# The mixed heads' norm in pieces beside the latent heads and the output projection, and the input projection's 32-token tile in four f32 parts

## The chip, the cores and the metric

The kernel runs on one core of one Trainium2 chip, as one launch that reads and writes HBM. The time is device microseconds of that core, as the median of the runs shown. The core has a matrix engine (PE, TensorE), whose weight loads are traced apart (PEld), a vector engine (DVE), a scalar engine (ACT), a general engine (POOL, GpSimd) and an engine that only issues transfers here (SP). Each has its own instruction queue and works it off in order; they meet at semaphores.

## The reference

One step of a streaming encoder with two layers. 1024 frames of a new stream and 32 frames of a running one make 1056 tokens of 1024 features. Cut to what matters:

```python
h = rmsnorm(x)                          # per token over 1024 features
cols = h @ w_in                         # 9 blocks of 246 columns: inputs of three kinds of heads
y_fox, y_swa, y_mla = ...               # attention; 6, 6 and 4 heads of 64 features
y = concat(rms(y_fox), rms(y_swa), rms(y_mla)) * g_mix_out     # "mixed heads' norm": each kind by itself
x = x + y @ w_out
x = x + ConvFFN(rmsnorm(x))             # 1024 -> 2816 -> 1024
# _rmsnorm: x * rsqrt(mean(x * x) + 1e-6) * g, all in float32
```

## The kernel before

Everything lies transposed in SBUF where it is multiplied: features on the 128 partitions in 8 chunks (`DC`), tokens along the free axis, in three thirds of 352 tokens (`NT`, `TN`). In the input projection tokens are taken in nine tiles: eight of 128 and one of 32 (the running stream's; number `QT` = 8). A product in nearly full precision is made of three reduced-precision (fp32r) matmuls: each operand is split into a high part (a copy that rounds, on ACT) and a low part (value minus high part, on POOL or DVE), and high x high, high x low and low x high are added in PSUM.

A layer is a row of stages, each an `nc.Block`, which ends when all engines are through with it. Inside, each engine's program is written out by hand, and semaphores order them. The stages of a layer: `ProjectIn` (w_in in 9 steps of 246 columns); `fox_rows`, `attend_prompt` and `attend_sample` for fox, then for swa; `mla_prepare`, which builds queries, keys and values of the latent (MLA) heads; `attend_prompt` and `attend_sample` for MLA, whose results are chunks 6 and 7 of `yT`; `restart`, in which POOL clears the semaphores for use by the next stages; `norm`; and `layer_out`, which holds `ProjectOut`, `ConvFFN` and, in layer 0, the next layer's `ProjectIn`, in one Block.

`ProjectIn` loads a block of raw weights per step (SP, `load`, L487 to L492; two buffers), ACT makes its high part (`split`, L509), POOL its low part (`low`, L500), and PE runs 8 chunks x 3 matmuls for each of nine tiles (L546). ACT evicts each tile scaled by its token's root (L523).

`norm` handles the three groups (fox is chunks 0 to 2, swa 3 to 5, MLA 6 to 7) third by third: squares on ACT and POOL, sums over partitions by a matmul with ones on PE (L395), Ln and Exp on ACT, scaling on DVE (L412), high part on ACT, low part on DVE and POOL. Its SP also starts the loads of w_out's first two blocks:

```python
    restart(nc, used)
    ...
        norm(nc, k, yT, y_hi, y_lo, k.vec[lay], V_GM, "2" + k.tag, [(0, 3), (3, 6), (6, 8)], first_blocks)
```

`ProjectOut` takes w_out in 8 blocks (`m`) x three thirds x 24 matmuls (L1807). Its ACT and POOL split a block (L1721, L1728); SP loads the blocks, and brings and stores the residual x.

At the end of layer 0's FFN, `Tail` makes the next layer's operand as columns of x are finished: for each of 24 pieces (128x352) DVE adds the last product (L2143) and, one piece later, makes a low part (`Tail.low_part`, L2206); ACT makes the high part and a square, POOL adds the squares. PE's next work is the first step of layer 1's `ProjectIn`.

## Time and profile before

| what | value |
|---|---|
| median of 3 runs | 3323.86 us (3323.02 to 3326.49) |
| the profiled execution's own time | 3319.49 us |
| its span | 3317.7 us |
| PE busy | 2993.8 us, 90% of the span |
| PEld / DVE / ACT / POOL busy | 84% / 47% / 30% / 26% |
| mean granted TensorE clock | 0.935 of full speed |

The stages and durations quoted later are from the profiled execution; it was 4.37 us shorter than the median. The busy share of PE is an average: most of the rest of the span lies in stretches in which PE waits for a stage's other engines.

### The profile page before, as it was taken

To read this page: it belongs to the slowest core of one execution; us is meant where nothing else is said; L and a number is where in the kernel's file an instruction comes from. 1 tells how busy PE (TensorE), PEld (TensorE's weight loads), DVE (VectorE), ACT (ScalarE), POOL (GpSimd) and SP (SyncE) were. 2 spreads that over 40 slices of the span, in tenths; PEclk is the share of its full clock that TensorE was granted. 3 is DMA by queue.
4 is the path that set the end of the run, shared out by engine and by line. 5 is a ranking of instruction groups with operands and counts; after the bars stand their busy time and mean duration, and the time that the engine had idled before them with its cause. 6 is when DMAs were issued, how large, how long until landed. Compare 5 with 4: busy or idle time off the path is not lost. (4 is left out here: it accounts for less than half of the span.)

```text
span 3317.7 us, 50480 instructions
## 1 busy us (share of the span) xinstructions
PE 2993.8 (90%) x19996; PEld 2799.5 (84%) x19996; DVE 1575.9 (47%) x2735; ACT 992.2 (30%) x2175; POOL 860.9 (26%) x488
## 2 busy tenths in 40 slices
PE   7998877677999999999999998867679999999998
PEld 6997755456999999999899975636479999999998
DVE  3336655734344444444441474657333444444443
ACT  4224535534311111111232253445433111111111
POOL 3112141113422232223331123311143232222230
PEclk9998968788999999999999997788889999999999
DMA  5110100002511111111131101000034111111111
GB/s 182 37 42 22 40 11 18 1 9 63 169 58 38 51 50 38 40 49 43 51 102 47 41 2 40 10 17 1 13 98 149 51 38 51 38 51 38 51 51 53
DMA packets 181248, 161.79 MB, mean 49 GB/s; under 512 B 17236, under 2 KB 168316, under 8 KB 180860
## 3 DMA queue, kind: packets, MB, share of 16 engines
q1 hardware_dynamic: 181116, 160.02, 15.6%
q8 instruction: 84, 1.38, 0.2%
q14 instruction: 48, 0.39, 0.0%
HBM read 129.97 MB, written 30.13 MB: 48 GB/s over the span
## 5 line engine op out<-in xcount | busy, mean ns | idle before, releaser
L1954 PE MATMUL bank_b<-x_hi,fwhi 128*128 128x352 f32 x2112 | 690.1, 327 | 5.3 <-POOL fwlo L1910 5.3
L1954 PE MATMUL bank_b<-x_hi,fwlo 128*128 128x352 f32 x2112 | 688.4, 326 | 0.0
L1954 PE MATMUL bank_b<-x_lo,fwhi 128*128 128x352 f32 x2112 | 686.7, 325 | 0.0
L1910 POOL TENSOR_TENSOR fwlo<-raw,fwhi 128x1024 fp32r<-128x1024 f32 x132 | 321.9, 2439 | 583.3 <-ACT fwhi L2035 569.2
L1954 PEld LDWEIGHTS bank_b<-x_hi,fwhi 128*128 128x128 f32 x2112 | 399.4, 189 | 6.5 <-POOL fwlo L1910 5.9
L1954 PEld LDWEIGHTS bank_b<-x_lo,fwhi 128*128 128x128 f32 x2112 | 401.7, 190 | 0.0
L1954 PEld LDWEIGHTS bank_b<-x_hi,fwlo 128*128 128x128 f32 x2112 | 398.4, 189 | 0.6
L2143 DVE TENSOR_TENSOR fx<-fx,bank_b 128x352 f32<-128x352 f32 x528 | 275.3, 521 | 233.5 <-PE bank_b L1984 233.5
L1984 PE MATMUL bank_b<-fuhi,fwhi 128*128 128x352 f32 x1056 | 344.1, 326 | 10.2 <-DVE fx L2143 5.7
L1984 PE MATMUL bank_b<-fulo,fwhi 128*128 128x352 f32 x1056 | 344.5, 326 | 0.0
L1984 PE MATMUL bank_b<-fuhi,fwlo 128*128 128x352 f32 x1056 | 344.0, 326 | 0.0
L2055 ACT ACTIVATE fuhi<-fcb 128x1024 fp32r<-128x1024 f32 x44 | 46.7, 1061 | 696.4 <-PE bank_b L1984 550.8
L1919 POOL TENSOR_TENSOR fcb<-fcb,rsb 128x1024 f32<-128x1024 f32 x44 | 97.0, 2203 | 511.2 <-ACT fcb L2049 511.2
L1984 PEld LDWEIGHTS bank_b<-fuhi,fwhi 128*128 128x128 f32 x1056 | 201.3, 191 | 13.9 <-DVE fx L2143 8.9
L1984 PEld LDWEIGHTS bank_b<-fulo,fwhi 128*128 128x128 f32 x1056 | 199.0, 188 | 0.0
L1984 PEld LDWEIGHTS bank_b<-fuhi,fwlo 128*128 128x128 f32 x1056 | 198.6, 188 | 0.0
L546 PE MATMUL bank_a<-whi,x_hi 128*128 128x246 f32 (+1 forms) x648 | 181.9, 281 | 13.5 <-POOL x_lo L321 11.3
L546 PE MATMUL bank_a<-whi,x_lo 128*128 128x246 f32 (+1 forms) x648 | 182.0, 281 | 0.0
L546 PE MATMUL bank_a<-wlo,x_hi 128*128 128x246 f32 (+1 forms) x648 | 182.0, 281 | 0.0
L546 PE MATMUL bank_b<-whi,x_lo 128*128 128x246 f32 (+1 forms) x648 | 180.6, 279 | 0.0
L546 PE MATMUL bank_b<-wlo,x_hi 128*128 128x246 f32 (+1 forms) x648 | 180.5, 278 | 0.0
L546 PE MATMUL bank_b<-whi,x_hi 128*128 128x246 f32 (+1 forms) x648 | 179.8, 277 | 0.1
(410 smaller groups left out, 5965.8 us busy)
## 6 DMA issues: line engine op xcount, KB each, us to landing
raw<-in_w_ffn_up SPq DMA_DIRECT2D x88, 512.0 KB, 3.9
raw<-in_w_ffn_down SPq DMA_DIRECT2D x44, 512.0 KB, 3.6
wraw<-in_w_in SPq DMA_DIRECT2D x18, 984.0 KB, 5.4
xs<-x_between SPq DMA_DIRECT2D x16, 528.0 KB, 4.1
x_between<-xs SPq DMA_DIRECT2D x16, 528.0 KB, 2.6
fx<-x_between SPq DMA_DIRECT2D x2, 4224.0 KB, 13.3
raw<-in_w_out SPq DMA_DIRECT2D x16, 512.0 KB, 5.3
x_between<-fx SPq DMA_DIRECT2D x3, 1408.0 KB, 6.3
```

Of the source, the lines that this page charges most:

```text
L546: last = pe.matmul(bank[0:n, t % NB, 0:WN], a[:, c, at], w[b][:, c, :], start=(c == 0 and m == 0), stop=(c == DC - 1 and m == 2))
L1910: pool.tensor_tensor(self.wlo[:, r], self.raw[:, o % 2], self.whi[:, r].bitcast(F32), ALU.subtract)\
L1919: pool.tensor_tensor(v, v, self.rsb[:, 0:SEQ], ALU.mult)
L1954: last = pe.matmul(bank[:, first_bank + t, 0:TN], w[:, role, c, :], x[:, c, self.cols(t)], start=(c == 0 and m == 0), stop=(c == DC - 1 an ...
L1984: last = pe.matmul(bank[:, 6 + o % 2, 0:TN], w[:, D0 + e, m, :], x[:, e, self.cols(t)], start=(e == 0 and i == 0), stop=(e == 1 and i == 2))
L2055: act.activation(uhi[:, e, 0:SEQ], cb[:, e, 0:SEQ], ACT.Copy)
L2143: dve.tensor_tensor(x, x, bank[:, 6 + o % 2, 0:TN], ALU.add).then_inc(self.p_out[o % 2], 1)
```

## The change

**Norm.** The stage `norm` goes, in both layers. A class `MixedNorm` does its work in other stages. The first six chunks (fox and swa): POOL squares and adds them in `mla_prepare` (10 instructions of 128x1056, `pool_squares`), followed there by 6 sums on PE and Ln and Exp on ACT. In the stage of `attend_prompt` for MLA 18 pieces (6 chunks x 3 thirds) are scaled on DVE, get a high part on ACT and a low part on POOL, one piece for each unit (head and block of queries) of the 24 units. The last two chunks (MLA's own result) are squared, summed, scaled and split at the beginning of `layer_out`, while PE multiplies chunks 0 to 5 for `m` = 0 and 1. The loads and splits of w_out's first two blocks move into `attend_sample` for MLA. `restart` moves from behind that stage to between `mla_prepare` and `attend_prompt` (it clears 97 semaphores instead of 103).

**Input projection.** The 32-token tile is multiplied in full-precision f32: the weights are the raw block `wraw`, its 246 columns in four parts of 62, 62, 62 and 60 (`PARTS`) that go to four groups of 32 PSUM partitions. An f32 matmul shows as two records in a trace, so there are 8 x 4 x 2 = 64 records where there were 24. The operand is high plus low part of the 32 tokens, added up by `vector_samples` on DVE. The raw buffer is now read by PE, so SP's next load waits for PE's last tile too. ACT evicts the tile in four pieces. PE's queue at the last tile of step 0, where `tok_lo` is the tokens' low parts and `win_tf2` a free PSUM bank; before (these three rows stand eight times):

```order
L546 MATMUL bank_a<-whi_90,x_hi 32x246 [waits win_tf2,tok_lo]
L546 MATMUL bank_a<-wlo_92,x_hi 32x246
L546 MATMUL bank_a<-whi_90,x_lo 32x246
```

and now (the last two rows repeat to the end of the tile):

```order
L595 MATMUL bank_a<-wraw_89,const 32x62 [waits win_xs,win_tf2,tok_lo]
L595 MATMUL bank_a<-wraw_89,const 32x62 x2
L595 MATMUL bank_a<-wraw_89,const 32x60
L595 MATMUL bank_a<-wraw_89,const 32x62 x3
L595 MATMUL bank_a<-wraw_89,const 32x60
```

The 32 tokens' operand (in `const`) comes from DVE (`win_xs`), and four parts follow each other for each chunk. SP's queue at the loads of w_in for steps 2 to 8 of layer 0, before (a loop; `win_lo0` says that a block's low part is made):

```order
L492 ISA [waits win_lo0]
L492 DMA wraw_88<-in_w_in 128x8x246
L492 ISA [waits win_lo1]
L492 DMA wraw_89<-in_w_in 128x8x246
L475 REGISTER_ALU
L475 COMPARE_AND_BRANCH
L492 DMA wraw_88<-in_w_in 128x8x246 [waits win_lo0]
```

and now (seven such rows, written out, and behind them the first load of another stage):

```order
L530 DMA wraw_89<-in_w_in 128x8x246 [waits win_done2,win_lo0]
L530 DMA wraw_90<-in_w_in 128x8x246 [waits win_done2,win_lo1]
...
L779 DMA fcl_55<-in_cache_fox_logf 128x8x6
```

Each load now also waits for `win_done2`, the end of the 32-token tile two steps before the one loaded, whose weights lie in the same buffer. PE's queue from the end of MLA's sample stage to the output projection, before:

```order
L1397 MATMUL psO_smla<-pT_smla,vm 128x64 x17
L1320 UNCONDITIONAL_BRANCH
L386 UNCONDITIONAL_BRANCH [waits barrier_Pool_Activation_PE_DVE_SP_release]
L395 MATMUL nps_0<-nsq_0,const 128x352 [waits norm_sq]
...
L351 UNCONDITIONAL_BRANCH
L2317 UNCONDITIONAL_BRANCH [waits barrier_Pool_Activation_PE_DVE_SP_release]
L1807 MATMUL bank_b<-y_hi_7907,fwhi_8056 128x352 [waits wout_lo0]
```

and now:

```order
L1467 MATMUL psO_smla<-pT_smla,vm 128x64 x17
L1384 UNCONDITIONAL_BRANCH
L2426 UNCONDITIONAL_BRANCH [waits barrier_Pool_Activation_PE_DVE_SP_release]
L1893 MATMUL bank_b<-y_hi_2114,fwhi_2123 128x352 [waits wout_lo0]
...
L468 MATMUL bank_b<-ylsq_2120,const 128x352 [waits mix_p] x2
L468 MATMUL bank_b<-ylsq_2120,const 128x352 [waits mix_ln,mix_p]
L1893 MATMUL bank_b<-y_hi_2114,fwhi_2123 128x352 [waits wout_lo1]
...
L1893 MATMUL bank_b<-y_hi_2114,fwhi_2123 128x352 [waits mix_lo]
```

The norm's sums and one barrier are gone from between the two stages; the last group's sums (L468) stand between the chunks 0 to 5 of `m` = 0 and those of `m` = 1, and the late chunks wait for that group's low parts (`mix_lo`).

**Places.** Buffers move: the residual x and the FFN's input low part lie elsewhere, and `Tail`'s low parts of the first third are made 16 adds behind (`BEHIND`) and those of the other two thirds after all adds (`vector_third`), each third after its x is stored.

The diff, cut to its core:

```diff
+    def pool_squares(self, pool):
+        own = Steps(pool, self.pool_steps, self.steps0)
+        for g, acc in enumerate(self.acc):
+            a, b, c = (self.y[:, 3 * g + n, :] for n in range(3))
+            own.after(pool.tensor_tensor(acc[:, :], a, a, ALU.mult))
+            own.after(pool.tensor_tensor(self.sq[0][:, :], b, b, ALU.mult))
+            own.after(pool.tensor_tensor(self.sq[1][:, :], c, c, ALU.mult))
+            own.after(pool.tensor_tensor(acc[:, :], acc[:, :], self.sq[0][:, :], ALU.add))
+            own.after(pool.tensor_tensor(acc[:, :], acc[:, :], self.sq[1][:, :], ALU.add))
...
+    def sums(self, pe, banks):
+        for n in range(self.GROUPS * NT):
+            g, t = divmod(n, NT)
+            pe.wait_ge(self.pool_steps, self.steps0 + 5 * (g + 1))
+            if n >= 2:
+                pe.wait_ge(self.logged, self.sums0 + n - 1)
+            pe.matmul(banks[:, n % 2, 0:TN], self.k.const[:, C_ONE:C_ONE + P], self.acc[g][:, self.cols(t)],
+                      start=True, stop=True).then_inc(self.summed, 1)
+    def scalar_roots(self, act, banks):
+        for n in range(self.GROUPS * NT):
+            g, t = divmod(n, NT)
+            act.wait_ge(self.summed, self.sums0 + n + 1)
+            act.activation(self.roots[:, g, self.cols(t)], banks[:, n % 2, 0:TN], ACT.Ln, scale=1.0 / (3 * P),
+                           bias=self.k.const[:, C_EPS:C_EPS + 1]).then_inc(self.logged, 1)
+        act.wait_ge(self.logged, self.sums0 + self.GROUPS * NT)
+        act.activation(self.roots[:, :, :], self.roots[:, :, :], ACT.Exp, scale=-0.5).then_inc(self.rooted, 1)
...
+    def vector(self, dve, n):
+        if 0 <= n < self.PIECES:
+            c, at = self.piece(n)
+            v = self.y[:, c, at]
+            dve.scalar_tensor_tensor(v, v, self.gain[:, c:c + 1], self.roots[:, c // 3, at], ALU.mult, ALU.mult)\
+                .then_inc(self.normed, 1)
+    def scalar(self, act, n):
+        if 0 <= n < self.PIECES:
+            c, at = self.piece(n)
+            act.wait_ge(self.normed, self.pieces0 + n + 1)
+            act.activation(self.hi[:, c, at], self.y[:, c, at], ACT.Copy).then_inc(self.hi_done, 1)
+    lowered = 0
+    def pool_upto(self, pool, upto):
+        for n in range(self.lowered, min(upto, self.PIECES)):
+            c, at = self.piece(n)
+            pool.wait_ge(self.hi_done, self.pieces0 + n + 1)
+            if n:
+                pool.wait_ge(self.lo_done, self.pieces0 + n)
+            pool.tensor_tensor(self.lo[:, c, at], self.y[:, c, at], self.hi[:, c, at].bitcast(F32), ALU.subtract)\
+                .then_inc(self.lo_done, 1)
+            self.lowered = n + 1
...
+    def last_scalar(self, act, bank):
+        k = self.k
+        for t in range(NT):
+            act.activation(self.last_sq[:, 0, self.cols(t)], self.y[:, self.EARLY, self.cols(t)], ACT.Square)\
+                .then_inc(self.act_sq, 1)
+        for t in range(NT):
+            act.wait_ge(self.summed, self.last_sums0 + t + 1)
+            act.activation(self.last_roots[:, self.cols(t)], bank[:, 6 + t % 2, 0:TN], ACT.Ln, scale=1.0 / (2 * P),
+                           bias=k.const[:, C_EPS:C_EPS + 1]).then_inc(self.logged, 1)
+        act.wait_ge(self.logged, self.last_sums0 + NT)
+        act.activation(self.last_roots[:, :], self.last_roots[:, :], ACT.Exp, scale=-0.5).then_inc(self.rooted, 1)
+        for n, t, c in self.last_pieces():
+            act.wait_ge(self.normed, self.last0 + n + 1)
+            act.activation(self.hi[:, c, self.cols(t)], self.y[:, c, self.cols(t)], ACT.Copy).then_inc(self.hi_done, 1)
...
+    def last_vector(self, dve):
+        for t in range(NT):
+            y = self.y[:, self.EARLY + 1, self.cols(t)]
+            dve.tensor_tensor(self.last_sq[:, 1, self.cols(t)], y, y, ALU.mult).then_inc(self.dve_sq, 1)
+        dve.wait_ge(self.rooted, self.roots0 + 2)
+        for n, t, c in self.last_pieces():
+            v = self.y[:, c, self.cols(t)]
+            dve.scalar_tensor_tensor(v, v, self.gain[:, c:c + 1], self.last_roots[:, self.cols(t)], ALU.mult, ALU.mult)\
+                .then_inc(self.normed, 1)
+        for n, t, c in self.last_pieces():
+            dve.wait_ge(self.hi_done, self.last0 + n + 1)
+            dve.tensor_tensor(self.lo[:, c, self.cols(t)], self.y[:, c, self.cols(t)],
+                              self.hi[:, c, self.cols(t)].bitcast(F32), ALU.subtract).then_inc(self.lo_done, 1)
...
+    PARTS = [(32 * g, 62 * g, min(62 * (g + 1), WN)) for g in range(4)]
...
-        def body(i, b, step):
-            if is_first(i):
-                return
+        for step in range(2, WSTEPS):
+            i, b = divmod(step, 2)
             sp.wait_ge(self.lo_done[b], i)
+            sp.wait_ge(self.tile_done[QT % self.NB], (step - 1) * self.per)
             sp.dma_start(self.raw[b][:, :, :], w_in_block(self.k, self.lay, step)).then_inc(self.raw_in[b], 16)
-        self.steps(sp, body)
...
-                act.activation(proj[0:n, t, col:col + WN], self.bank[0:n, t % NB, 0:WN], ACT.Copy,
-                               scale=k.rs1[0:n, t:t + 1]).then_inc(self.tile_free[t % NB], 1)
+                parts = [(0, 0, WN)] if t < QT else self.PARTS
+                for p, a, z in parts:
+                    last = act.activation(proj[0:n, t, col + a:col + z], self.bank[p:p + n, t % NB, 0:z - a], ACT.Copy,
+                                          scale=k.rs1[0:n, t:t + 1])
+                last.then_inc(self.tile_free[t % NB], 1)
...
+                    if t == QT:
+                        if c == 0 and is_first(step):
+                            pe.wait_ge(self.samples_in, 1)
+                        for p, a, z in self.PARTS:
+                            last = pe.matmul(bank[p:p + n, t % NB, 0:z - a], self.samples[:, c, :],
+                                             self.raw[b][:, c, a:z], start=(c == 0), stop=(c == DC - 1))
+                        continue
...
+                if beside:
+                    pool.wait_ge(pool_normed, len(shared))
+                    beside.pool_upto(pool, NU)
...
+                    if beside:
+                        beside.scalar(act, m - 3)
...
+                if weights:
+                    weights.load_w(sp, 0)
+                    weights.load_w(sp, 1)
...
+                pool.wait_ge(zeroed, 4)
+                mixed.pool_squares(pool)
...
+    def slot(self, m):
+        return m if m < 2 else 2 + m % 2
+    def split_behind(self, m):
+        return (2,) if m == 0 else (3,) if m == 1 else (m + 1,) if 3 <= m < DC - 1 else ()
...
+        early, late = range(mixed.EARLY), range(mixed.EARLY, DC)
+        for m in range(2):
+            pe.wait_ge(self.lo_w[m], 1)
+            for t in range(NT):
+                third(m, t, early)
+            if m == 0:
+                mixed.last_sums(pe, bank)
+        for m in range(2):
+            for t in range(NT):
+                mixed.last_split(pe, t)
+                third(m, t, late).then_inc(self.tile_done[m], 1)
+        for m in range(2, DC):
             b = m % 2
             pe.wait_ge(self.lo_w[b], m // 2 + 1)
             for t in range(NT):
-                if m >= 2:
-                    pe.wait_ge(self.added[b], (m // 2 - 1) * NT + t + 1)
-                at = slice(t * TN, (t + 1) * TN)
-                for c in range(DC):
...
     def low_part(self, dve, o):
         m, at = self.place(o)
+        if m == 0:
+            dve.wait_ge(self.x_stored[o // DC], 16)
         dve.wait_ge(self.hi_done, o + 1)
+        dve.wait_ge(self.squared, o + 1)
         dve.scalar_tensor_tensor(self.k.lo[:, m, at], self.ffn.xT[:, m, at], self.gain[:, m:m + 1],
                                  self.k.hi[:, m, at].bitcast(F32), ALU.mult, ALU.subtract).then_inc(self.lo_done, 1)
     def vector(self, dve, o):
-        if o:
-            self.low_part(dve, o - 1)
-        if o == self.O - 1:
+        if o >= self.BEHIND:
+            self.low_part(dve, o - self.BEHIND)
+    def vector_third(self, dve, t):
...
                 else:
                     ffn.vector(dve, lambda o: tail.vector(dve, o))
+                    tail.vector_third(dve, 1)
                     front.vector(dve)
+                    tail.vector_third(dve, 2)
+                    dve.wait_ge(tail.lo_done, tail.O)
+                    pin.vector_samples(dve)
...
+        mla_prepare(nc, k, lay, places, proj, qm, km, vm, mixed)
+        restart(nc, used)
         left.close()
-        attend_prompt(nc, k, "mla", MLAH, MQK, lambda h: qm[:, :, h, :], lambda h: km[:, :, h, :],
-                      lambda h, t: vm[:, t, h, :], lambda h: h, yT, 6)
+        with ExitStack() as f2:
+            keep(f2, "y_early", mixed.EARLY * places.CHUNK)
+            attend_prompt(nc, k, "mla", MLAH, MQK, lambda h: qm[:, :, h, :], lambda h: km[:, :, h, :],
+                          lambda h, t: vm[:, t, h, :], lambda h: h, yT, 6, beside=mixed)
...
-    restart(nc, used)
-    y_lo = places.at("y_lo" + k.tag, [P, DC, TOK], places.XT, F32R)
-    y_hi = places.at("y_hi" + k.tag, [P, DC, TOK], places.Y_HI, F32R)
-    raw = places.at("raw" + k.tag, [P, 2, DC, P], places.RAW)
-    def first_blocks(sp):
-        for b in range(2):
-            sp.dma_start(raw[:, b], w_out_block(k, lay, b)).then_inc(k.sems["wout"]["raw"][b], 16)
-    with ExitStack() as f:
-        keep(f, "y_kept", places.LOW)
-        norm(nc, k, yT, y_hi, y_lo, k.vec[lay], V_GM, "2" + k.tag, [(0, 3), (3, 6), (6, 8)], first_blocks)
+                      [], yT, 6, weights=pout)
     right.close()
```

## Rows read from the trace of the kernel before

**Rows 1.** The page: engines' busy time; POOL's 128x1024 additions (busy us, mean ns).
```profile
PE 2993.8 (90%) x19996; PEld 2799.5 (84%) x19996; DVE 1575.9 (47%) x2735; ACT 992.2 (30%) x2175; POOL 860.9 (26%) x488
...
L1919 POOL TENSOR_TENSOR fcb<-fcb,rsb 128x1024 f32<-128x1024 f32 x44 | 97.0, 2203 | 511.2 <-ACT fcb L2049 511.2
```

**Rows 2.** Windows: input projection, MLA prompt, norm, output projection, MLA sample.
```profile
core 0: us, PE busy (x) PEld busy (x) DVE busy (x) ACT busy (x) POOL busy (x), PEclk, DMA share, GB/s
65.00:264.00 199.00, 199.00 (x1723) 198.23 (x1722) 72.09 (x89) 52.73 (x90) 31.69 (x7) 1.00 0.17 51
617.00:705.00 88.00, 80.55 (x672) 69.41 (x672) 55.91 (x120) 48.80 (x135) 10.03 (x8) 0.91 0.00 1
733.00:785.00 52.00, 17.16 (x48) 10.26 (x48) 23.66 (x28) 29.03 (x29) 18.33 (x7) 0.66 0.12 31
785.00:881.00 96.00, 95.54 (x579) 95.55 (x580) 28.77 (x46) 29.69 (x53) 40.73 (x32) 0.97 0.39 123
724.00:728.00 4.00, 4.00 (x18) 3.88 (x18) 0.00 (x0) 0.00 (x0) 0.00 (x0) 0.50 0.00 0
```

**Rows 3.** Timeline, MLA prompt to output projection: start, us, instruction, [idle before].
```profile
705.11 0.28 ACT L1164 ACTIVATE yT<-psOmla 128x128 f32<-128x128 f32 x1 [2.20 <-PE psOmla L1117]
...
707.36 0.34 PE L1344 MATMUL psQ_smla<-const,qm 32*96 32x32 f32 x4 [2.29 <-PEq L2364]
...
732.51 0.41 DVE L1480 COPY yT<-psO_smla 64x32 f32<-64x32 f32 x2 [3.81 <-PE psO_smla L1397]
...
742.69 0.99 SPq L2496 DMA_DIRECT2D raw<-in_w_out  x2
...
756.89 4.97 PE L395 MATMUL nps<-nsq,const 128*128 128x352 f32 x16 [0.56 <-ACT nsq L362]
...
759.52 1.28 ACT L372 ACT_TABLE_LOAD   x1
760.82 1.08 ACT L372 ACTIVATE nrs<-nrs 128x1056 f32<-128x1056 f32 x1
...
761.93 0.58 DVE L412 SCALAR_TENSOR_TENSOR nhf<-yT,vec,nrs 128x352 f32<-128x352 f32 x1 [2.36 <-ACT nrs L372]
...
785.46 0.66 PE L1807 MATMUL bank_b<-y_hi,fwhi 128*128 128x352 f32 x1 [23.59 <-POOL fwlo L1728]
```

**Rows 4.** Waits between 617 and 705 us: waiting, releaser, us in total, times, longest.
```profile
ACT qThimla L1127 <- PE psXmla L1053: 27.3, 13, 14.4
...
DVE stmla L1198 <- PE psSmla L1084: 17.5, 18, 2.4
```

**Rows 5.** Timeline of POOL and DVE in `mla_prepare`.
```profile
603.94 5.54 POOL L1536 TENSOR_TENSOR km<-km,mhs 128x3072 f32<-128x3072 f32 x1 [51.20 <-ACT mhs L1545]
604.22 8.88 DVE L1630 TENSOR_TENSOR qm<-qm,mhs 128x3456 f32<-128x3456 f32 x1
613.13 3.76 DVE L1631 TENSOR_TENSOR qm<-qm,row 128x3456 f32<-128x3456 f32 x1
```

**Rows 6.** Timeline of PE where it makes f32 products of few columns.
```profile
703.11 1.97 PE L1117 MATMUL psOmla<-pTmla,vm 128*64 128x128 f32 x32 [0.83 <-ACT pTmla L1143]
...
715.65 1.98 PE L1371 MATMUL psS_smla<-kT_smla,qz_smla 96*32 96x352 f32 x24 [0.33 <-issue]
...
723.99 4.26 PE L1397 MATMUL psO_smla<-pT_smla,vm 128*128 128x64 f32 x18 [0.58 <-DVE pT_smla L1303]
```

**Rows 7.** Timeline of ACT in the input projection, at the turn of a step.
```profile
215.11 1.83 ACT L509 ACTIVATE whi<-wraw 128x1968 fp32r<-128x1968 f32 x1
...
217.53 0.47 ACT L523 ACTIVATE proj<-bank_a,rs 128x246 f32<-128x246 f32 x1 [0.59 <-PE bank_a L546]
```

**Rows 8.** The view of line L492, SP's w_in loads: from issue to landing.
```profile
DMA to landing us min/median/max: 5.1/5.4/9.6
```

**Rows 9.** Timeline of the FFN's last matmuls in layer 0, with what POOL did.
```profile
1645.22 4.34 POOL L500 TENSOR_TENSOR wlo<-wraw,whi 128x1968 fp32r<-128x1968 f32 x1 [5.93 <-ACT whi L509]
...
1650.42 0.66 PE L1984 MATMUL bank_b<-fuhi,fwhi 128*128 128x352 f32 x1 [4.88 <-DVE fx L2143]
```

279 lines of the change are left out of this document (132 added, 147 removed).

## The prediction, made before the changed kernel had run

> **What bounds the kernel now.** I read the page first: PE is busy 90% of the span [rows 1], so a gain comes either from PE's own work or from the stretches in which PE waits for other engines. The windows tell these apart [rows 2]. In the input projection (65 to 264 us) PE is busy without a break at full granted clock: 1723 matmuls in 199 us, 115.5 ns each. What shortens PE's work there shortens the kernel. The output projection (785 to 881 us) is just as full. Between 733 and 785 us, the norm, no engine is busy for more than 29 of 52 us: the stage is a chain through all of them. In the MLA prompt stage (617 to 705 us) PE is busy for 80.6, DVE 55.9, ACT 48.8, POOL 10.0 of 88 us. Last I read the timeline across the norm [rows 3]: MLA's last result is copied at 732.51 + 0.41 = 732.92; then POOL clears semaphores, and SP and the norm's engines start at 742.69; the first matmul of the output projection follows at 785.46, released by POOL's low part of w_out's block.
>
> All sums are against the profiled execution, 3319.49 us, which lies 4.37 under the median of the runs shown (3323.86); at the end I add 4.37. Layer 1 has the same stages, so a layer's terms count twice.
>
> **The norm's stage goes.** From 732.92 to 785.46 are 52.54 us. A usual boundary of stages, from MLA prompt's last copy (705.11 + 0.28) to MLA sample's first matmul at 707.36, costs 1.97 [rows 3]. So 50.57 a layer goes: -101.1.
>
> **The restart is moved, not removed.** It took 742.69 - 732.92 = 9.77 us with the boundaries on both its sides [rows 3]. At its new place it replaces a boundary of 1.97, so it adds 7.80, or scaled to 97 of 103 semaphores 7.35. It is a stage by itself, and nothing runs beside it. Twice: +14.7.
>
> **What the norm's work costs where it goes.** Where rows give only bounds, I take a value between them.
>
> *18 pieces in MLA prompt.* A piece is a DVE instruction of 0.58 us, as the scaling in the norm [rows 3], a copy on ACT and a subtraction on POOL of that size. DVE is free for 32 of the 88 us, ACT for 39, POOL for 78 [rows 2]. What counts is what stands behind a piece in its queue. DVE waits 18 times for scores, 17.5 us together, about 1 us each; ACT waits 27.3 us for transposed queries, 14.4 of it once [rows 4]. A piece of 0.6 mostly fits into a wait of 1. With no cover it would be 18 x 0.59 = 10.6 a layer, with full cover 0. The waits are the nearer rows: I take 2, so +4.
>
> *POOL's squares in `mla_prepare`.* Ten instructions of 1056 columns, by POOL's 2203 ns for 1024 [rows 1] 2.27 us each, 23 us. POOL idles for 51.2 us ahead of its large instruction at 603.94 [rows 5], and that is their cover; without it they would cost up to 23. DVE is disturbed only where the two meet: its product of 3456 columns took 8.88 us beside POOL's of 5.54, and 3.76 alone [rows 5]. The squares fill only the first 23 of those 51 us, where DVE has short copies; one can wait for one square. 0 to 2.2, I take 1.2: +2.4.
>
> The Trainium skill ("SBUF — State Buffer", Who interferes with whom) puts such pairs down to a port that DVE and GpSimd share as an exclusive lock when a DVE instruction reads two inputs from SBUF. The 8.88 against 3.76 agrees. The rule speaks against the pieces in MLA prompt: scaling reads two inputs and would wait for a POOL subtraction that it meets. At 2203 ns x 352/1024 = 0.76 us and 18 meetings that is 13.6 a layer instead of 2, +23 and 3246 in all, an estimate. It needs each piece to meet POOL's; I keep it inside rival 2, which ends above it.
>
> *w_out's first two blocks in MLA sample.* ACT and POOL split them there instead of before the output projection; the stage's own chain goes through PE, ACT and DVE. At worst a POOL instruction of a block holds one DVE instruction, 2.4 with its wait; at best nothing. I take 0.5: +1.
>
> *The last group in the output projection.* PE gets three sums. Sixteen records of that shape took 4.97 us [rows 3], two records a sum: 0.62, 1.9 a layer, +3.8. The rest of the chain has PE's early chunks as cover: 54 matmuls for `m` = 0, 54 for `m` = 1, at 95.54 us for 579 [rows 2], 165 ns, 8.9 us each. Squares and additions need three rounds of 0.5 to 0.8 ahead of the sums and lie well inside the first 8.9. Behind the sums come a logarithm of half a microsecond, a table load of 1.28, the exponential of 1.08, six scalings of 0.58 and two low parts of about 0.58 [rows 3]: 7.5, under the second 8.9 by 1.4. Without that cover the chain would cost 7.5 a layer. What may stall also is w_out's next blocks, whose loads stand behind other issues on SP. 0 to 7, I take 1.5, near the covered end: +3.
>
> **The 32-token tile.** Before: 24 matmuls of 115.5 ns [rows 2], 2.77 us. Now: 64 records of 60 or 62 columns with 32 columns of weights. No row shows such a tile. From below: the sample's scores are f32 with 32 weight columns too, four groups in turn; 24 records of 352 columns took 1.98 [rows 6], 0.33 for a round of four. At 62 columns that is 0.058, and 16 rounds 0.93. From above: the prompt's output products, with 64 weight columns, 32 records in 1.97 [rows 6], 61.6 ns a record; 64 of these 3.94. The form is that of the first row, but its records are long, and short ones show whatever it costs to start one. I take half again the low end, 1.4: 9 tiles x 2 layers x (2.77 - 1.4) = -24.7. The ends are -33.1 and +21.1.
>
> The Trainium skill ("TensorEngine Tiling (Array Packing)", Key Properties) says that such tiles load weights and multiply in parallel; its section Instruction Overhead gives some 60 cycles for each matmul. At 2.4 GHz, one after another, that would be 25 ns x 64 = 1.6 us, an estimate, and the term -21. No row here has records short enough to show it.
>
> The raw block must now stay until this tile is multiplied. So SP's next load starts with the next step's tile 0, lands 5.4 us later (5.1 to 9.6) [rows 8], ACT splits it in 1.83 and only then evicts tile 0 in 0.47 [rows 7]: 7.7 us. PE needs that bank (of three) for tile 3, after 3 x 2.77 = 8.31. At the median landing it is hidden by 0.6 us; I cost it at nothing. If the cover is gone, each load's excess counts, 14 times. ACT's three more evictions a step fit into its idle time (busy for 52.73 of 199 us [rows 2]).
>
> **FFN's end, layer 0.** PE waited 4.88 us there for one DVE addition, which stood behind a low part while POOL's instruction of 4.34 ran [rows 9]. With low parts 16 additions behind, additions run free. Late next are the low parts of the second and third thirds: eight of 0.58 [rows 3] are 4.7 us, against two tiles of 2.77 that PE has before it needs them; the third third comes the same way. About 1 us may show: 0 to -4.9, I take -4.
>
> **Sum.** -101.1 + 14.7 + 4 + 2.4 + 1 + 3.8 + 3 - 24.7 - 4 = -100.9: 3218.6 for the profiled execution, 3223 as a median. With every bounded term at its good end, -101.1 + 14.7 + 3.8 - 33.1 - 4.9 = -120.6, 3203. A measurement of this kernel can tell about 0.2%, 6.6 us, from no change.
>
> **Rivals.**
> 1. *Short records have a floor.* If each costs 61.6 ns, whatever its length, the tile takes 3.94: 18 x 2.54 = +45.8, 3269. For it: no row has a record much shorter. Against: that row streams 128 columns with two groups, not 62 with four. 12 in 100.
> 2. *The pieces land on the path.* All of 10.6 in MLA prompt, 2.2 in `mla_prepare`, 2.4 in MLA sample and 7 in the output projection: 22.2 a layer instead of 5.2, +34, 3257. For it: each piece stands in front of something in a queue worked off in order; and if the last group's chain holds up the late chunks, the norm has not left the path. Against: the waits of [rows 4] and the 1.4 us to spare. 12 in 100.
> 3. *The raw loads come late.* At 9.6 us to landing, a step loses 9.6 + 1.83 + 0.47 - 8.31 = 3.6; 14 times 50, 3273. For it: 9.6 occurred [rows 8]. Against: it is the longest, and 5.4 the median. 5 in 100.
> 4. *Slower than before.* The four parts don't overlap, and each record pays what the sample's last products pay: 18 records in 4.26 us, 237 ns at a granted clock of 0.50 [rows 2, 6], 118 at full clock. The tile then takes 7.6 us, 18 x 6.2 = +112: 3335. It decides from a tile of 7.0 us on, 109 ns a record, where 18 x 5.6 eats the 100.9. Against: that row loads 128 columns of weights for each record, ours 32. 3 in 100.
>
> **Chances and range.** The forecast is 3223, with a range of its own of 3200 (3203 less the runs' own scatter) to 3243, 68 in 100. The range of 8 in 10 takes in rival 2: 3200 to 3260. All cases but the fourth are faster by more than 0.2%, so 0.96; within 0.2% 0.01; slower 0.03.
>
> **What the new profile would show.** PE's first output matmul some 2 us after MLA sample's last copy, and some 10 us between `mla_prepare`'s last instruction and MLA prompt's first. The tile's 64 records within 1 to 1.7 us, a step of the input projection 23.6 us instead of 24.9, and PE not waiting for ACT's eviction at tile 3. MLA prompt 88 to 91 us long. Three short sums in the output projection with no wait of more than 1.5 us around them, and no wait of 4.9 us at FFN's end. The prediction is wrong if the tile takes over 2 us, if MLA prompt grows by more than 5, or if PE waits at tile 3 of the projection's steps.

## The result, and the profile after

The changed kernel takes 3231.09 us (median of 4 runs, 3227.81 to 3234.66) against 3325.16 for the one before (4 runs): a ratio of 0.9718, with a 95% interval of 0.9702 to 0.9733. Forecast were 3223, with 3200 to 3260 as the range. The profiled execution took 3231.43 us (span 3229.7); the spans differ by 88.0, where the sum said 100.9. (The medians differ by 94.1; the profiled execution of before was 5.7 under the median here, that of after beside its own.) Its first page row stands against [rows 1]:

```profile
PE 2960.0 (92%) x20656; PEld 2770.8 (86%) x20656; DVE 1578.2 (49%) x2747; ACT 999.4 (31%) x2259; POOL 919.6 (28%) x538
```

I split both traces at the same landmarks (a stage's last result, or the first matmul of the next one) and subtracted. "Forecast" is the prediction's term.

| term, both layers together | forecast, us | measured, us |
|---|---|---|
| MLA's last copy to the first output matmul (52.54 and 52.06 before; 2.14 and 1.85 now) | -101.1 | -100.6 |
| restart at its new place (a boundary of 0.30 before; 7.07 and 6.77 now) | +14.7 | +13.2 |
| MLA prompt with 18 pieces (+1.44, +2.27) | +4 | +3.7 |
| `mla_prepare` with the squares (+0.53, -0.78) | +2.4 | -0.3 |
| MLA sample with w_out's splits (+0.79, +1.28) | +1 | +2.1 |
| output projection: sums and waits (+5.64, +7.40) | +6.8 | +13.0 |
| input projection, first matmul to the next stage (-8.44, -7.30) | -24.7 | -15.7 |
| FFN of layer 0, to the projection's first matmul | -4 | -5.9 |
| stages that the change does not touch | 0 | +2.4 |
| sum | -100.9 | -88.0 |

**The norm left and the restart came.** The timeline of after, two places in it; compare [rows 3]:

```profile
607.75 3.76 DVE L1709 TENSOR_TENSOR qm<-qm,row 128x3456 f32<-128x3456 f32 x1
...
618.59 0.42 PE L1112 MATMUL psXmla<-const,qm 128*96 128x128 f32 x1 [13.60 <-PEq L2477]
...
736.14 0.41 DVE L1553 COPY yT<-psO_smla 64x32 f32<-64x32 f32 x2 [3.81 <-PE psO_smla L1467]
...
738.69 0.63 PE L1893 MATMUL bank_b<-y_hi,fwhi 128*128 128x352 f32 x1 [2.59 <-PEq L2477]
```

From 736.55 to 738.69 there is only a boundary. From `mla_prepare`'s last DVE instruction, 611.51, to MLA prompt's first matmul at 618.59 no engine computes, and PE's wait names its own sequencer at the line of `restart`. The view of the line that clears semaphores says what that stretch holds, and what the stretch of 9.77 us held before; before, then after:

```profile
L2369 POOLq EVENT_SEMAPHORE_RANGE_CLEAR  x123: 44/44/44, 733.2 to 742.3; - x123
```

```profile
L2482 POOLq EVENT_SEMAPHORE_RANGE_CLEAR  x97: 37/38/38, 611.7 to 618.2; - x97
```

The 123 are the 103 of `restart` and 20 of the attention stage that ended just ahead of it.

**MLA prompt.** Waits of after between 618 and 708 us, then DVE's group of scalings there (busy us, mean ns); compare [rows 4]:

```profile
ACT qThimla L1187 <- PE psXmla L1113: 21.4, 11, 10.8
...
DVE stmla L1260 <- PE psSmla L1144: 8.5, 11, 1.9
...
PE psTmla L1164 <- POOL prmla L1098: 0.8, 2, 0.4
```

```profile
L401 DVE SCALAR_TENSOR_TENSOR yT<-yT,vec,yrs 128x352 f32<-128x352 f32 x18 | 13.5, 748 | 0.0
```

The 18 scalings took 13.5 us of DVE, and DVE's waits for scores fell from 17.5 to 8.5: the pieces lie mostly in those waits, as the prediction had it. (The two fences are the views of waits and of lines.) The mean of 748 ns mixes lengths: in layer 0 eleven pieces take 0.57 or 0.58 us, as the norm's did; two that start beside a subtraction take 0.67; and five of the six that start beside POOL's product for the heads' probabilities (L1098) take 1.02 to 1.33. One of these in the timeline:

```profile
637.94 1.89 POOL L1098 TENSOR_TENSOR prmla<-prmla,stmla 128x1024 f32<-128x1024 f32 x1 [1.28 <-DVE stmla L1266]
...
638.89 1.32 DVE L401 SCALAR_TENSOR_TENSOR yT<-yT,vec,yrs 128x352 f32<-128x352 f32 x1
```

PE's waits inside the stage grow by only 0.8 us in each layer, from 7.3 to 8.1, and they are those for that product. The rest of the stage's growth is PE itself, busy longer with the same number of records.

**The 32-token tile.** Timeline of after: a tile in the steady steps, the first one with what DVE and POOL did, and ACT at a late load; then the window behind that first tile:

```profile
59.01 4.38 POOL L537 TENSOR_TENSOR wlo<-wraw,whi 128x1968 fp32r<-128x1968 f32 x1
...
59.70 3.97 DVE L551 TENSOR_TENSOR const<-x_hi,x_lo 128x256 f32<-128x256 f32 x1
...
63.82 1.07 PE L595 MATMUL bank_a<-wraw,const 128*32 128x62 f32 x64 [2.70 <-DVE const L551]
...
88.85 1.07 PE L595 MATMUL bank_a<-wraw,const 128*32 128x62 f32 x64
...
1711.89 1.85 ACT L546 ACTIVATE whi<-wraw 128x1968 fp32r<-128x1968 f32 x1 [2.19 <-DMA wraw<-in_w_in]
...
1714.29 0.38 PE L599 MATMUL bank_b<-whi,x_hi 128*128 128x246 f32 x1 [0.87 <-ACT proj L568]
```

```profile
64.50:69.50 5.00, 5.00 (x57) 4.91 (x47) 3.81 (x2) 1.23 (x4) 0.00 (x0) 0.66 0.66 199
```

The tile takes 1.07 us, shorter than I took it for, and a steady step 23.48 us instead of 24.99. But in layer 0's first step PE waits 2.70 us for the samples' sum, an instruction of 0.43 us in layer 1 that took 3.97 beside POOL's of 4.38. Behind that wait the granted clock is 0.66 for 5 us (half for the first tile: 4.44 us instead of 2.79). This does not always follow: in the traces of `w_ahead_one`, `pieces_doubled` and `squares_short`, below, the same tile waits 2.7 us too, and the granted clock behind it is 1.00; in `w_ahead_one`:

```profile
65.50 1.07 PE L595 MATMUL bank_a<-wraw,const 128*32 128x62 f32 x64 [2.69 <-DVE const L551]
```

```profile
66.50:71.50 5.00, 5.00 (x49) 5.00 (x44) 3.79 (x2) 1.23 (x4) 0.00 (x0) 1.00 0.67 202
```

So 1.5 us of what the changed kernel's trace loses there is the clock's, and does not come with every such wait.

One step in layer 1 waits 0.87 for a late raw load (1711.89 to 1714.29), ahead of its tile 3; others wait less. The loads' view, against [rows 8]:

```profile
DMA to landing us min/median/max: 5.0/5.3/6.8
```

At the end of each layer's input projection nothing runs beside ACT's eviction of the tile. Timeline of before, then of after:

```profile
264.72 0.46 ACT L523 ACTIVATE proj<-bank_a,rs 32x246 f32<-32x246 f32 x1 [2.23 <-PE bank_a L546]
```

```profile
254.90 1.26 ACT L568 ACTIVATE proj<-bank_a,rs 32x62 f32<-32x62 f32 x4 [0.57 <-PE bank_a L595]
```

The four pieces take 0.8 us longer than the one did, and the last step gains 0.44 us in layer 0 and 0.78 in layer 1 instead of 1.51.

**The output projection.** Timeline of after: the three sums, then what precedes block 4 (`m` = 4), and the same wait in layer 1 with the window behind it:

```profile
750.02 2.32 PE L468 MATMUL bank_b<-ylsq,const 128*128 128x352 f32 x6
...
780.78 0.32 SPq L1799 DMA_DIRECT2D x_between<-xs  x1
783.45 0.32 SPq L1784 DMA_DIRECT2D xs<-x_between  x1
783.82 0.43 SPq L1787 DMA_DIRECT2D raw<-in_w_out  x1
...
789.11 1.06 ACT L1809 ACTIVATE fwhi<-raw 128x1024 fp32r<-128x1024 f32 x1 [5.72 <-DMA raw<-in_w_out]
...
790.25 2.35 POOL L1817 TENSOR_TENSOR fwlo<-raw,fwhi 128x1024 fp32r<-128x1024 f32 x1 [5.39 <-ACT fwhi L1809]
...
792.66 0.43 PE L1893 MATMUL bank_b<-y_hi,fwhi 128*128 128x352 f32 x1 [2.36 <-POOL fwlo L1817]
...
2383.03 0.66 PE L1893 MATMUL bank_b<-y_hi,fwhi 128*128 128x352 f32 x1 [2.36 <-POOL fwlo L1817]
```

```profile
2383.00:2386.00 3.00, 2.97 (x10) 2.97 (x11) 1.54 (x3) 0.98 (x2) 3.00 (x3) 0.50 0.95 317
```

The late chunks' chain is hidden, as forecast. What stalls is block 4: SP issues its load at 783.82, behind the store of x (780.78) and the load of x (783.45); it lands, is split, and PE goes on 2.36 us late, in both layers. In layer 1 half clock follows.

**FFN's end.** Timeline of after, from the last additions to layer 1's first tiles; compare [rows 9]:

```profile
1626.27 8.35 POOL L2335 TENSOR_TENSOR rsb<-rsb,sqo 128x352 f32<-128x352 f32 x7
...
1627.07 8.93 DVE L2315 SCALAR_TENSOR_TENSOR x_lo<-fx,vec,x_hi 128x352 fp32r<-128x352 f32 x9
...
1628.04 0.35 PE L599 MATMUL bank_b<-whi,x_hi 128*128 128x246 f32 x1 [1.72 <-DVE x_lo L2315]
...
1636.05 2.10 PE L713 MATMUL bank_b<-const,rsb 128*128 128x1 f32 x18 [0.69 <-DVE x_lo L2315]
```

The wait of 4.88 us is gone. PE now waits 1.72 us ahead of the first tile and again ahead of the sums, both times for a low part: nine of them take 8.93 us on DVE while POOL adds squares. From the start of FFN's last matmul to the third tile's it was 7.65 us before, and is 12.08 now.

### The profile page after: what moved, and what is told of

Its sections match the earlier page's. It is cut to its first block and busy times, and to the rows that moved or that the text cites. A ratio compares the mean times of both kernels' runs of the same rounds, so it can differ in the third digit from the quotient of the medians.

```text
span 3229.7 us, 51941 instructions
## 1 busy us (share of the span) xinstructions
PE 2960.0 (92%) x20656; PEld 2770.8 (86%) x20656; DVE 1578.2 (49%) x2747; ACT 999.4 (31%) x2259; POOL 919.6 (28%) x538
## 5 line engine op out<-in xcount | busy, mean ns | idle before, releaser
L2059 PE MATMUL bank_b<-f_lo,fwhi 128*128 128x352 f32 x2112 | 685.9, 325 | 0.0
L2059 PEld LDWEIGHTS bank_b<-f_lo,fwhi 128*128 128x128 f32 x2112 | 401.1, 190 | 0.0
L599 PE MATMUL bank_a<-whi,x_hi 128*128 128x246 f32 x576 | 163.9, 284 | 13.4 <-POOL x_lo L324 10.9
L599 PE MATMUL bank_b<-whi,x_hi 128*128 128x246 f32 x576 | 162.6, 282 | 3.0 <-DVE x_lo L2315 1.7
L599 PE MATMUL bank_a<-wlo,x_hi 128*128 128x246 f32 x576 | 162.8, 283 | 0.0
L599 PE MATMUL bank_a<-whi,x_lo 128*128 128x246 f32 x576 | 162.7, 282 | 0.0
L599 PE MATMUL bank_b<-whi,x_lo 128*128 128x246 f32 x576 | 162.2, 282 | 0.0
L599 PE MATMUL bank_b<-wlo,x_hi 128*128 128x246 f32 x576 | 162.1, 281 | 0.0
```

What stands on the lines that cost most here:

```text
L599: last = pe.matmul(bank[0:n, t % NB, 0:WN], a[:, c, at], w[b][:, c, :], start=(c == 0 and m == 0), stop=(c == DC - 1 and m == 2))
L2059: last = pe.matmul(bank[:, first_bank + t, 0:TN], w[:, role, c, :], x[:, c, self.cols(t)], start=(c == 0 and m == 0), stop=(c == DC - 1 an ...
```

## The experiments

All are edits of the changed kernel. Times are medians; those without an interval are from a single execution.

**tile_undone**, the 32-token tile as it was:

```diff
-                    if t == QT:
...
-                        for p, a, z in self.PARTS:
-                            last = pe.matmul(bank[p:p + n, t % NB, 0:z - a], self.samples[:, c, :],
-                                             self.raw[b][:, c, a:z], start=(c == 0), stop=(c == DC - 1))
-                        continue
...
-            sp.wait_ge(self.tile_done[QT % self.NB], (step - 1) * self.per)
```

> The changed kernel with the 32-token tile as it was before (24 split matmuls, no sum of the samples, no wait of the loads for the tile); the norm stays as changed. Theory: a step of the input projection is 24.99 us with the old tile and 23.48 with the new one where nothing waits, 1.51 a step, but in layer 0's first step the new tile waits 2.7 us for the samples' sum and the next tile runs at half clock, so layer 0 gains 9 rather than 13.6, and layer 1 nearly 13. Undone, the time rises by 17 to 24 us over the changed kernel's 3231, and the gap ahead of layer 0's last tile of step 0 is gone. Rival: the first step's end is set by the low part of the second block of weights, which POOL ends at 63.4 us whatever the tile does; then the step 1 starts at the same place with either tile, and what undoing costs is 8 x 1.51 in layer 0, not 9.

3252.25 us, ratio 0.9776 (0.9754 to 0.9798): 21 more than the changed kernel. Layer 0's projection takes 249.0 us as before, against 240.6; layer 1's 233.0 against 221.9. The theory's total held (17 to 24), and its parts nearly (9 and nearly 13 were said, 8.4 and 11.1 came); the rival's 12.1 for layer 0 did not come. So the tile, with the waits that came with it, is worth about 20 us of the 94. The rest is the norm's move for the most part, and FFN's end.

**restart_split**, semaphores cleared by four engines:

```diff
-        @block.gpsimd
-        def _(pool):
-            for x in sems:
-                pool.sem_clear(x)
+        def part(n):
+            return lambda eng: [eng.sem_clear(x) for x in sems[n::4]]
+        block.gpsimd(part(0))
+        block.vector(part(1))
+        block.scalar(part(2))
+        block.sync(part(3))
```

> The changed kernel with the semaphores of each restart cleared by four engines (POOL, DVE, ACT, SP), a quarter each, instead of by POOL alone. Theory: the restart now costs its length, 6.8 us between mla_prepare's last instruction and MLA prompt's first against 0.3 before, and nothing hides it; 97 clears go one after another. With 25 on each engine the gap falls to 2.5 to 4 us, 3 to 4 a layer, 6 to 9 us in all. Rival: a clear goes through something that the engines share, or the stage's two barriers are the cost; then the gap stays above 6 and the time does not move.

3211.07 us, ratio 0.9660 (0.9644 to 0.9676), 20 less, more than twice what I expected. Its timeline at the restart:

```profile
604.87 3.76 DVE L1709 TENSOR_TENSOR qm<-qm,row 128x3456 f32<-128x3456 f32 x1
```

```profile
611.25 0.42 PE L1112 MATMUL psXmla<-const,qm 128*96 128x128 f32 x1 [8.96 <-PEq L2477]
```

608.63 to 611.25 are 2.62 us instead of 7.07: 8.6 for both layers, as the theory had it. What I had left out: the attention stages also end with such a clear, of their own semaphores. There are twelve, with 20 semaphores each; their boundaries fall from mostly 1.84 us to mostly 1.04, by some 10 us in all. They stood in the kernel before too, so this part of the gain has nothing to do with the change. MLA prompt, up to its last copy, is 2.3 us shorter a layer besides, with the granted clock at 0.69 instead of 0.56 in its second 7 us; that the shorter idle stretch ahead is the reason is argued, not tested. PE's waits inside the stage are 8.1 us here as in the changed kernel. So, with all its 18 pieces, the stage takes 87.4 and 87.6 us to its last copy, against 88.2 and 87.3 in the kernel before: the clock moves it as much as the pieces do.

**w_ahead_one**, loads of w_out one place earlier on SP:

```diff
+        next_block(0)
         for m in range(DC):
-            sp.wait_ge(self.lo_w[m % 2], m // 2 + 1)
-            if m + 2 < DC:
-                self.load_w(sp, m + 2)
-            else:
-                load_next(sp, m % 2)
+            if m + 1 < DC:
+                next_block(m + 1)
```

(`next_block` holds the removed lines.)

> The changed kernel with each load of a w_out block one place earlier in SP's queue, ahead of the store of x and the load of x that it stood behind. Theory: block 4's load is issued at 783.8 us because the store before it waits until block 1 of x is finished, and lands, is split and lets PE go on 2.7 us late in each layer; in layer 1 the clock falls to half behind that wait. With the load at about 770 the wait is gone: 2.7 in layer 0, 2.7 + 2.3 in layer 1, 7 to 8 us in all. Rival: PE's wait is for POOL, which would be late with block 4's low part anyway, since it adds the squares of x ahead of it; then the wait stays above 1.5 us.

3225.78 us, ratio 0.9705 (0.9688 to 0.9723): 5 less, with intervals of the ratio that overlap, so the trace has to decide. The load for block 4 is issued 30.6 us after the first output matmul (741.05) instead of 45.1:

```profile
771.62 0.43 SPq L1787 DMA_DIRECT2D raw<-in_w_out  x1
```

and no gap of PE is left in the output projection beside the sums. From its first matmul to FFN's first it takes 98.24 and 98.28 us, against 100.79 and 102.34. The theory holds, at 6.6 us for both layers, a little under its 7 to 8; the wait behind POOL that the rival expected is not there.

**samples_pool**, layer 0's sum of the 32 tokens on POOL:

```diff
-                dve.wait_ge(ld.lo_done, TT)
-                pin.vector_samples(dve)
...
+                pool.wait_ge(ld.lo_done, TT)
+                pin.vector_samples(pool)
                 pin.pool(pool, 1)
```

> The changed kernel with layer 0's sum of high and low parts of the 32 tokens made by POOL, ahead of its low part of the second block of weights, instead of by DVE beside it. Theory: the 2.7 us wait at the first 32-token tile is DVE's instruction of 0.43 us, which took 3.97 beside POOL's of 4.38; with the sum on POOL the wait is below 0.5 us, and the next tile does not fall to half clock: 3 to 4.5 us less. Rival: the low part of the second block ends at 63.4 and, moved back by the sum, at 64 us; step 1 cannot start earlier, the wait only moves behind the tile, and the gain is 0.5 to 1 us.

3236.38 us, ratio 0.9729 (0.9712 to 0.9747): nothing gained. The rival is right:

```profile
61.94 4.38 POOL L537 TENSOR_TENSOR wlo<-wraw,whi 128x1968 fp32r<-128x1968 f32 x1
```

```profile
63.13 1.07 PE L595 MATMUL bank_a<-wraw,const 128*32 128x62 f32 x64
66.38 0.38 PE L599 MATMUL bank_a<-whi,x_hi 128*128 128x246 f32 x1 [2.18 <-POOL wlo L537]
```

The wait ahead of the tile is gone and stands behind it, for the next block's low part. From the third tile of step 0 to the start of step 2 it takes 54.38 us, 0.8 less than in the changed kernel (55.21), and here the granted clock behind the wait stayed at full.

**w1_early**, that low part too moved, in two halves behind POOL's tokens 5 and 6, the split on ACT one tile earlier:

```diff
-    splits_at = 5
+    splits_at = 4
...
                 for t in range(1, TT):
                     ld.low(pool, t)
-                pin.pool(pool, 1)
+                    if 5 <= t < 7:
+                        pin.low_half(pool, t - 5)
+                pool.wait_ge(ld.lo_done, TT)
+                pin.vector_samples(pool)
+                pin.pool(pool, 2)
```

> The changed kernel with, in layer 0's first projection step, the low part of the second block of weights made in two halves ahead of POOL's last two low parts of tokens (ACT splits that block one tile earlier), and the sum of the 32 tokens on POOL behind them. Theory: with the sum alone on POOL the wait only moved behind the tile, to step 1, because that block's low part was late; with both early, PE meets neither wait, step 1 starts 1 us after the 32-token tile, at full clock: 3 to 4.5 us less than the changed kernel. Rival: the first step is a chain through ACT, and the earlier split only delays the next tokens' high parts by its 1.83 us: the waits move to tiles 5 to 7 and the gain is under 1.5 us.

3234.69 us, ratio 0.9724 (0.9708 to 0.9741), not to be told from the changed kernel. In the trace both waits are gone:

```profile
62.95 1.07 PE L605 MATMUL bank_a<-wraw,const 128*32 128x62 f32 x64
63.95 0.38 PE L609 MATMUL bank_a<-whi,x_hi 128*128 128x246 f32 x1
```

and from the third tile of step 0 to the start of step 2 it takes 51.44 us instead of 55.21, 3.8 less, as the theory said. Some 1.5 of the 3.8 is the half clock of the changed kernel's trace; against `w_ahead_one`, which has the same wait at full clock, it is 54.37 and the gain 2.9. Ahead of that third tile PE waited 1.4 us longer than in the changed kernel's trace, where ACT waits for a transfer of x; from the second tile's start to the third's it was 11.6 to 13.2 us in the traces of this study, whatever the edit.

**parts_two and parts_one**, the tile in two parts or one:

```diff
-    PARTS = [(32 * g, 62 * g, min(62 * (g + 1), WN)) for g in range(4)]
+    PARTS = [(32 * g, 123 * g, 123 * (g + 1)) for g in range(2)]      # parts_two
+    PARTS = [(0, 0, WN)]                                              # parts_one
```

> The changed kernel with the 32-token tile in two parts of 123 columns (two groups of 32 PSUM partitions) instead of four of 62. In the changed kernel the four-part tile takes 1.07 us for 64 records. Theory: parts in different groups run beside each other, and a tile takes its columns divided by the number of groups; two parts then take twice as long, 1.8 to 2.1 us for 32 records, and a step of the projection 24.3 to 24.5 us. Rival: a record costs a fixed 15 to 17 ns, however long; then 32 records take 0.55 us and a step 23.0.

> The changed kernel with the 32-token tile in one f32 part of 246 columns. Theory (columns divided by groups): 16 records one after another, four times the four-part tile less its overhead, 3.3 to 4 us, which is longer than the 2.70 of the split tile before: full precision by itself gains nothing, the four groups gain it. Rival (a fixed cost for each record): 16 records in 0.3 us. A step of the projection is 25.7 to 26.4 us by the theory and below 23.5 by the rival.

3242.89 and 3271.06 us. The tile in the timelines of parts_two, then parts_one:

```profile
90.20 1.88 PE L595 MATMUL bank_a<-wraw,const 128*32 128x123 f32 x32
```

```profile
91.50 3.51 PE L595 MATMUL bank_a<-wraw,const 128*32 128x246 f32 x16
```

Steps of 24.30 and 25.91 us. The theory holds twice: the time goes roughly with columns divided by groups, 3.51, 1.88, 1.07 us, and the steps' lengths differ by as much as the tiles'. A cost per record is refuted: four times the records take less than a third of the time. In one part the tile is slower than the split one of before.

**pieces_doubled**, DVE's scaling made twice:

```diff
+            dve.scalar_tensor_tensor(self.hi[:, c, at], v, self.gain[:, c:c + 1], self.roots[:, c // 3, at],
+                                     ALU.mult, ALU.mult)
             dve.scalar_tensor_tensor(v, v, self.gain[:, c:c + 1], self.roots[:, c // 3, at], ALU.mult, ALU.mult)\
```

> The changed kernel with DVE's scaling of each of the 18 pieces in MLA prompt made twice (first into the place of the high part, which ACT then overwrites, then as it was). Theory: a DVE piece fits into DVE's waits for scores, and MLA prompt, from its first matmul to the next stage's (91.6 us in layer 0, 91.9 in layer 1), grows by 0 to 2.5 us with the second set. Rival: DVE's queue is what the stage hangs on, and each further 0.58 us is paid: 10 us a layer.

3260.70 us, and my theory falls: MLA prompt grows by 13.8 and 12.7 us a layer. Waits and DVE's two groups:

```profile
DVE stmla L1262 <- PE psSmla L1146: 8.2, 7, 2.3
```

```profile
L403 DVE SCALAR_TENSOR_TENSOR yT<-yT,vec,yrs 128x352 f32<-128x352 f32 x18 | 16.5, 918 | 0.0
L401 DVE SCALAR_TENSOR_TENSOR y_hi<-yT,vec,yrs 128x352 fp32r<-128x352 f32 x18 | 13.3, 736 | 0.0
```

The second set adds 16.3 us to DVE (13.3, and 3 more on the first), and next to none of it went into DVE's waits: those for scores stay at 8.2 where the first set had brought them from 17.5 to 8.5. What cover there was, the first set had used up. The 13.8 us in layer 0 are of two kinds, as the windows of the changed kernel and of this one show:

```profile
618.00:708.00 90.00, 81.31 (x672) 69.80 (x672) 67.26 (x138) 55.45 (x153) 29.36 (x26) 0.91 0.01 1
```

```profile
620.00:724.00 104.00, 87.38 (x672) 73.96 (x672) 81.35 (x156) 57.33 (x154) 30.25 (x26) 0.87 0.00 1
```

PE waits 7.7 us longer inside the stage (for DVE's copies `pTmla` 8.8 instead of 3.2), and it is busy 6.1 us longer with the same 672 records, at a lower granted clock. How much of the growth would stay at the clock of before is not shown.

**lows_sooner**, low parts 14 additions behind:

```diff
-    BEHIND = 2 * DC
+    BEHIND = 14
...
-        for o in range(DC * t, DC * (t + 1)):
+        for o in range(max(DC * t, self.O - self.BEHIND), DC * (t + 1)):
```

> The changed kernel with Tail's low parts 14 additions behind instead of 16. At FFN's end in layer 0 the changed kernel's PE waits 2.04 us for a low part before layer 1's first tile, and again for the sums of squares after the second. Theory: the low parts are what is late, and with two more made beside the additions the second wait does not grow: layer 1's third tile starts 9.5 to 10.5 us after FFN's last matmul instead of 11.9. Rival: the chain of squares (ACT) and their additions (POOL) sets the third tile's start; PE starts the first tile 1 to 2 us earlier and waits that much longer ahead of the sums, and the third tile starts 11.5 to 13 us after FFN's last matmul.

3235.07 us. Layer 1's first tile follows FFN's last matmul with no wait, but the third starts 11.38 us after it (12.08 in the changed kernel). The wait moved to the sums, yet its releaser is again a low part, not POOL:

```profile
1641.55 3.06 PE L713 MATMUL bank_b<-const,rsb 128*128 128x1 f32 x18 [2.49 <-DVE x_lo L2315]
```

The time lies near the rival's 11.5 to 13 and far from the theory's 9.5 to 10.5, but neither had the cause by itself.

**squares_short**, POOL's additions of squares over 32 columns instead of 352:

```diff
-                pool.tensor_tensor(acc, acc, sq, ALU.add).then_inc(self.squares_added, 1)
+                pool.tensor_tensor(acc[:, 0:32], acc[:, 0:32], sq[:, 0:32], ALU.add).then_inc(self.squares_added, 1)
```

> The changed kernel with POOL's 21 additions of squares at FFN's end in layer 0 cut from 352 columns to 32 (so most of the row sums for layer 1's norm are left out). Theory: POOL's additions, 1.1 to 1.2 us each against 0.97 us from one FFN addition to the next, are what makes the sums late, and they also slow DVE's low parts beside them (0.84 instead of 0.58 us); cut, there is no wait ahead of the sums, the low parts take 0.58 us, and layer 1's third tile starts 7 to 8.5 us after FFN's last matmul instead of 12. Rival: ACT's part of that chain (a high part and a square for each addition, 1.08 us) is as late as POOL's, and the third tile starts 10.5 us or more after it.

3227.86 us. DVE's nine low parts and the sums:

```profile
1625.74 4.55 DVE L2315 SCALAR_TENSOR_TENSOR x_lo<-fx,vec,x_hi 128x352 fp32r<-128x352 f32 x9
```

```profile
1632.09 2.00 PE L713 MATMUL bank_b<-const,rsb 128*128 128x1 f32 x18
```

The low parts take 0.57 us each instead of up to 1.27 (4.55 for nine, 8.93 in the changed kernel), the sums wait for nothing, and the third tile starts 9.07 us after FFN's last matmul, 3 less. It is half a microsecond above the theory's 8.5; the wait ahead of the first tile stays at 1.20 (1.72 in the changed kernel), and its cause was not tested. So what holds the sums up is DVE's low parts growing longer beside POOL's additions.

**combined** (restart_split, w_ahead_one and w1_early together) and **after_again** (the changed kernel) on one chip:

> The changed kernel with three edits together: semaphores cleared by four engines, w_out loads one place earlier in SP's queue, and the second block's low part in two early halves with the samples' sum on POOL. Theory: they act in different places, and their gains add up: 19 us for the clears, 6 for the loads, 3 to 4 for the first step, so 3200 to 3206 us against the changed kernel's 3231. Rival: part of it is taken back where the gains meet other waits (the first step's gain was not seen in the time of its own run), and the time stays above 3208.

> The changed kernel itself, beside the combined one on the same chip. Expected: 3226 to 3236 us.

Combined 3206.70 us, ratio 0.9646 (0.9633 to 0.9659); the changed kernel beside it 3236.54, ratio 0.9733 (0.9715 to 0.9751). 29.8 less, so the combined kernel beats both the changed one and the one before. The three gains add up (28 to 29 were said) as far as executions of the changed kernel from 3229.43 to 3245.39 us can tell, and both times lie some half a microsecond above what was expected.

## Why the prediction held, and where its steps failed

- **The norm's stage, MLA prompt, the squares:** right in mechanism, and in size to within 3 us each. In MLA prompt 1.6 of the 3.7 are new waits of PE; the rest is PE's busy time, which `restart_split` shows to move with the granted clock. DVE's pieces did grow beside POOL, to 1.02 to 1.33 us, but beside its products for the heads; only two of 18 started beside a subtraction. The Trainium skill's rule ("SBUF — State Buffer", Who interferes with whom) agrees with these rows. The estimate worked out from it, 13.6 a layer, did not come (1.44 and 2.27), for it took every piece to meet a subtraction.
- **The restart:** the term came near, 13.2 for 14.7, by two errors that cancel, and that is luck. The stretch is 7.07 and 6.77 us long instead of the 9.3 that the sum implies (7.35 and 1.97), because the 9.77 of before held 123 clears and not 103. And the boundary that it replaced cost 0.30 and not 1.97, since `mla_prepare` clears no semaphores at its end.
- **The last group in the output projection:** the step failed is "I take 1.5, near the covered end". Its chain is hidden, but w_out's fourth block was late by 2.36 us in each layer, and in layer 1 half clock came after. With the sums the term is 13.0 instead of 6.8. I had named the place (loads behind other issues on SP), and the measured term lies between its two ends; `w_ahead_one` showed that the order on SP was the cause of that wait. It gave back 6.6 of the 13.0. Of the rest the sums are 4.6 (2.3 a layer instead of 1.9), and the cause of the last 1.8 is not shown.
- **The 32-token tile:** mis-sized upwards in time, 1.4 against 1.07, and the mechanism is right: parts in different groups run beside each other. The Trainium skill says so too ("TensorEngine Tiling (Array Packing)", Key Properties). The estimate that the prediction worked out from the Trainium skill ("TensorEngine Tiling (Array Packing)", Instruction Overhead), 1.6 us with the records one after another, did not come: 1.07.
- **What that tile gives:** the step that failed is that I multiplied a tile's gain by all 18 tiles: 15.7 came instead of 24.7, though a steady step gained 1.51, more than the 1.37 forecast. In layer 0's first step the end is set by POOL, not by PE: the samples' sum or, behind it, the next block's low part. That step gained nothing, and the one after it lost its gain to half clock. I had costed the new DVE instruction at nothing and not looked at what POOL does beside it. In layer 1's first step FFN's end took the gain. In each layer's last step ACT's eviction in four pieces took 0.8 of it back, which I had put at nothing too, since ACT has idle time inside the steps.
- **The raw loads:** the margin of 0.6 us was about as thin as said. Most landings, 5.3 us at the median, are hidden; the longest, 6.8, cost the 0.87 shown, in front of tile 3. That is one of the signs that the prediction had named for being wrong, in one step of 18: its zero for the loads was a little too low.
- **FFN's end:** FFN gave 5.9, and the next projection's first step, 29.49 us against 27.31, took 2.2 back in spite of its shorter tile. "About 1 us may show" was the failing step: eight low parts at 0.58 would have been hidden, but they took up to 1.27 beside POOL.
- **Rivals:** 1 and 4 are refuted by the tile, 3 is seen with at most 1.7 us of its 50 (steps of 23.81 and 24.82 where 23.47 is the usual), and of 2 only the output projection's part came, and there from w_out's load and not from the last group's chain.

## What to carry to other kernels

A stage that is one chain through all engines is worth its whole length when its work fits into other stages' waits, but that cover is spent once: the second set of pieces found none, and half clock came on top of its waits. When PE's work in a step shrinks, multiply the gain only by the steps that PE's work bounds, and look up what each engine does beside every small instruction that is added. Count what is paid at every boundary (here semaphore clears on one engine): clearing on four engines was worth as much as the faster tile.

## What the runs showed that I had not expected

- Four column groups of 32 run f32 matmuls of 62 columns at 64 records in 1.07 us, 17 ns a record; in one group a record of 246 columns takes 219 ns.
- Clearing 97 semaphores on one engine, with its boundaries, took 7.07 us; on four engines 2.62. A stage end with 20 took 1.84 and 1.04.
- A wait of 2.36 us in the middle of full work was followed by half clock in layer 1 (0.50 in the window from 2383 us) and not in layer 0, where the granted clock stayed at 1.00; in `restart_split` the same wait, 2.49 and 2.52, was followed by it in neither layer. The wait of 2.7 ahead of the first 32-token tile was followed by it in four of seven traces with that tile and that order (the changed kernel's two, `restart_split`, `lows_sooner`). What decides is not to be seen from these runs.
